# Token-major projections: the eight decode rows in float32 on four column groups of the matrix engine, and the semaphores cleared as one range

## What is computed

```
mod = silu(c) @ w_ada + b_ada                  # one row for the prompt, eight for the decode tokens
h   = rms_norm(x) * (1 + scale) + shift        # 520 x 1024
z   = h @ w_in                                 # 520 x (2048 retention + 1536 attention + 1824 RWKV + 3072 gates)
...                                            # three token mixers, gates, merge, squared-ReLU MLP
```

## Time and profile before

| what | value |
|---|---|
| time, median of 3 runs | 3102.15 us (3101.63 to 3105.66) |
| span of the profiled execution, first to last instruction | 3092.7 us |
| median run less the span | 9.45 us |
| PE busy | 2704.7 us, 87% of the span |
| DVE busy | 1464.7 us, 47% |
| ACT busy | 820.6 us, 27% |
| POOL busy | 162.0 us, 5% |

### The profile page before, as it was taken

The page is one execution under the profiler, slowest core; times in us unless marked ns, Lnnn a source line. Parts: engine busy times, 40 slices in busy tenths (PEclk is TensorE's granted clock), DMA queues, the critical chain, the costliest instruction groups (busy, mean ns, idle before and its releaser), DMA issues. The chain is left out here.

```text
span 3092.7 us, 53427 instructions
## 1 busy us (share of the span) xinstructions
PE 2704.7 (87%) x22862; PEld 2389.3 (77%) x22862; DVE 1464.7 (47%) x2073; ACT 820.6 (27%) x1218; POOL 162.0 (5%) x102
## 2 busy tenths in 40 slices
PE   5988888997698898999969879888967979799997
PEld 3777775886588698999958768567946859799997
DVE  3344346434655665334351541744366566633443
ACT  1221214223311323333222111332241114333331
POOL 0011110300000000000000210112000000000000
PEclk9997999996599799999979879999956989899999
DMA  6222345721000341222341330656010015322232
GB/s 257 98 59 58 113 134 185 228 72 52 14 3 3 126 177 66 98 82 83 137 148 35 86 120 23 219 183 200 16 52 15 3 44 178 110 83 82 83 110 109
DMA packets 216310, 305.16 MB, mean 99 GB/s; under 512 B 28021, under 2 KB 97191, under 8 KB 214786
## 3 DMA queue, kind: packets, MB, share of 16 engines
q1 hardware_dynamic: 216066, 301.67, 29.0%
HBM read 266.49 MB, written 35.14 MB: 98 GB/s over the span
## 5 line engine op out<-in xcount | busy, mean ns | idle before, releaser
L379 PE MATMUL pb<-h_high,f_high 128*128 128x260 f32 x1984 | 401.5, 284 | 4.9 <-DVEq L2619 4.9
L379 PE MATMUL pb<-h_low,f_high 128*128 128x260 f32 x1984 | 398.6, 282 | 0.0
L379 PE MATMUL pb<-h_high,f_low 128*128 128x260 f32 x1920 | 387.7, 283 | 0.0
L554 DVE TENSOR_TENSOR w_low<-ring,w_high 128x2048 fp32r<-128x2048 f32 x66 | 151.3, 2293 | 405.7 <-ACT w_high L546 404.3
L379 PEld LDWEIGHTS pb<-h_high,f_high 128*128 128x128 f32 x1984 | 306.5, 188 | 5.3 <-issue 5.3
L379 PEld LDWEIGHTS pb<-h_low,f_high 128*128 128x128 f32 x1984 | 307.6, 189 | 0.0
L554 DVE TENSOR_TENSOR f_low<-ring,f_high 128x2048 fp32r<-128x2048 f32 x60 | 137.6, 2293 | 339.1 <-ACT h_high L548 214.2
L379 PEld LDWEIGHTS pb<-h_high,f_low 128*128 128x128 f32 x1920 | 294.5, 188 | 0.0
L757 POOL TENSOR_TENSOR g_low<-yT,g_high 128x512 fp32r<-128x512 f32 x96 | 159.9, 1670 | 1978.0 <-ACT g_high L753 1978.0
L379 PE MATMUL pb<-w_high,h_high 128*128 128x512 f32 x560 | 224.9, 402 | 20.9 <-DVEq L558 11.7
L379 PE MATMUL pb<-w_low,h_high 128*128 128x512 f32 x560 | 224.2, 400 | 0.0
(11 more groups left out here) (362 smaller groups left out, 4620.2 us busy)
## 6 DMA issues: line engine op xcount, KB each, us to landing
ring<-in_w_ff_dram SPq DMA_DIRECT2D x32, 2048.0 KB, 7.8
ring<-in_w_in_dram SPq DMA_DIRECT2D x20, 2048.0 KB, 9.1
ring<-in_w_ada_dram SPq DMA_DIRECT2D x18, 2048.0 KB, 8.1
yT<-in_w_in_dram SPq DMA_DIRECT2D x96, 256.0 KB, 3.6
arena<-in_w_ada_dram SPq DMA_DIRECT2D x9, 2048.0 KB
gate_spill_dram<-yT SPq DMA_DIRECT2D x48, 260.0 KB, 4.0
arena<-gate_spill_dram SPq DMA_DIRECT2D x12, 1040.0 KB, 5.4
arena<-in_cache_k_diff_dram SPq DMA_DIRECT2D x32, 256.0 KB, 3.1
```

What stands on the lines that cost most here:

```text
L379: return PE.matmul(out, lhsT, rhs, start=start, stop=stop, skip_group_check=True)
L554: t = V.tensor_tensor(ws[n % 2][1], ring[slot][:, u * 2048:(u + 1) * 2048], ws[n % 2][0].bitcast(F32), sub)
```

## The change

The decode rows leave the five-tile loop. At the layer's start DVE puts the 8 decode columns of `h` in float32 into `h_dec`, padded to 32 columns with zeros. After the first half of each block PE makes eight float32 products of `h_dec` with the unsplit weights in the ring slot, on four column groups, into bank 4 (`dec_parts`). ACT copies bank 4 to `dec_stage`; after the second half PE sums the four groups by one float32 product with `fold` into bank 5, and ACT copies that out in place of tile 4. Since PE now reads the ring slot, DVE frees it only after `dec_parts`. The second part: `clear()` becomes one instruction over a range of 119 semaphores (two are new).

```diff
...
+        sem_numbers = sorted(s.num for s in sems.values())
+        assert sem_numbers == list(range(sem_numbers[0], sem_numbers[0] + len(sems)))
...
-                    for s in sems.values():
-                        g.sem_clear(s)
+                    g.sem_clear(range(sem_numbers[0], sem_numbers[-1] + 1))
...
+            h_dec = at(rstd, 0, KD, 32)
+            dec_count = {"made": Count(dec_made), "staged": Count(dec_staged), "read": Count(dec_made)}
...
                 dv(V.tensor_tensor(ht[:, :, SEQ:T], ht[:, :, SEQ:T], modT[:, 0:8, 1:9], add))
+                V.memset(h_dec[:, :, DEC:32], 0.0)
+                dv(V.tensor_copy(h_dec[:, :, 0:DEC], ht[:, :, SEQ:T]))
                 v.wait_ge(act_for_dve, c["dve_from_act"].next())
...
+                        def dec_parts(b):
+
+                            w = wslot(b % 2)
+                            for k in range(KD):
+                                g = slice(k % 4 * 32, k % 4 * 32 + 32)
+                                t = mm(pb[4][g, :], h_dec[:, k, :], w[:, k, :], start=(k < 4), stop=(k >= 4))
+                            t.then_inc(dec_made, 1)
+
...
-                                pe.wait_ge(act_for_pe, c["pe_from_act"].next(5))
-                                for k in range(5):
+                                pe.wait_ge(act_for_pe, c["pe_from_act"].next(4))
+                                for k in range(4):
                                     pe.wait_ge(h_ready, k + 1)
-                                    for m in range(4 if k < 4 else 0):
-                                        product(0, m, k)
-                                    if k:
-                                        t = product(0, 4, k - 1)
-                            for m in (() if before and n == 0 else range(5)):
+                                    for m in range(4):
+                                        t = product(0, m, k)
+                            for m in (() if before and n == 0 else range(4)):
...
                             if u == 0:
                                 t.then_inc(split_free, 1)
+                                dec_parts(n // 2)
+                            else:
+                                pe.wait_ge(dec_staged, dec_count["staged"].next())
+                                pe.wait_ge(act_for_pe, c["pe_from_act"].next())
+                                mm(pb[5][0:DEC, :], fold[:, 0:DEC], dec_stage).then_inc(pe_for_act, 1)
...
                                 split_hi(s, w_split, 2 * b + 2, (b + 1) % 2, 0)
+                            s.wait_ge(dec_made, dec_count["made"].next())
+                            S.activation(dec_stage, pb[4], ACT.Copy).then_inc(dec_staged, 1)
                             for m in range(5):
...
-                                                      pb[m][0:r, :], ACT.Copy))
+                                                      pb[m if m < MT else 5][0:r, :], ACT.Copy))
...
-                            split_lo(v, w_split, n, n // 2 % 2, n % 2, last=(n % 2 == 1))
+                            split_lo(v, w_split, n, n // 2 % 2, n % 2, last=False)
+                            if n % 2:
+                                v.wait_ge(dec_made, dec_count["read"].next())
+                                V.sem_inc(slot_free[n // 2 % 2], 1)
...
```

More of the change, by code:

```diff
@@ L311, in build @@
             "x_copied", "ba_made", "ba_masked", "br_made", "br_masked", "ka_made", "ka_masked", "kr_made", "kr_masked",
-            "x_made", "w_made", "w_masked", "x_added", "y_made", "y_added", "rhs_made", "rhs_copied", "u_made", "u_copied", "update_made", "state_read",
+            "dec_made", "dec_staged", "x_made", "w_made", "w_masked", "x_added", "y_made", "y_added", "rhs_made", "rhs_copied", "u_made", "u_copied", "update_made", "state_read",
             "state_done", "out_made", "out_copied")}
+        sem_numbers = sorted(s.num for s in sems.values())
+        assert sem_numbers == list(range(sem_numbers[0], sem_numbers[0] + len(sems)))
         chunk_scores, chunk_weighted, decode_added = sems["chunk_scores"], sems["chunk_weighted"], sems["decode_added"]
@@ L320, in build @@
         out_copied = sems["out_copied"]
+        dec_made, dec_staged = sems["dec_made"], sems["dec_staged"]
         pe_for_dve, dve_for_pe = sems["pe_for_dve"], sems["dve_for_pe"]
@@ L801, in build, with token_major @@
             upper = ((4, 5), (6, 7))
-            def token_major(col0, n_blocks, n_split, gates=False, before=None):
+            def token_major(col0, n_blocks, n_split, dec_stage, gates=False, before=None):
                 with nc.Block() as block:
@@ L918, in heads_to_columns @@
                 return pe_part, dve_part
-            token_major(RET0, 4, 1, gates=True, before=(start_sp, start_pe, start_s, start_v))
+            token_major(RET0, 4, 1, y_raw[:, 0:512], gates=True, before=(start_sp, start_pe, start_s, start_v))
             Z = lambda b: at(arena, b * 2560, 5, 512)
@@ L1125, in _ @@
                     pe_part(pe)
-            token_major(DIFF0, 3, 0)
+            token_major(DIFF0, 3, 0, x_raw[:, 0:512])
             w_ada_rest = L("w_ada")[:, 4 * 512:12 * 512]
```

## The result

Beside runs of the kernel before on the same chip, the changed kernel takes 3055.98 us (median of 4 runs, 3050.3 to 3057.57) against 3103.9 us (4 runs): ratio 0.9863, interval 0.9844 to 0.9883. It is faster, by 48 us. The forecast was 62.4 us less; the ratio laid on the 3102.15 us that the forecast started from gives 3059.6, outside 3029 to 3056. The ratios are given as recorded, and they are not the quotients of the medians: here that would be 0.9846, by which the time is 3054.3, just inside the range. In the other comparisons the two are up to 4 us apart. So the time missed narrowly, and a difference of under some 5 us can't be read from one comparison.

The account below looks back on a forecast made before the run. PE, busy for 87% of a 3092.7 us span, was taken as the bound, plus clears with nothing beside them. Terms -25.2 - 78.1 + 25.9 + 14.0 + 1.0 = -62.4 us took 3102.15 to 3040 us; range 3029 to 3056.

Parts of the forecast that it names:

- The clears: Three places of semaphore clears: one range clear each at 0.1 us instead of 8.6, 8.5 and 8.3; 25.2 us less.
- The tile removed: Decode tile in `token_major`: 24 products gone in each of 14 blocks, 5.58 us a block, 78.1 us less.
- `dec_parts`: Eight float32 products on column groups after each first half: 1.85 us x 14, 25.9 us more.
- that rival: Column groups don't overlap in `dec_parts`: 7.4 us each, +78 us over 14 blocks, 3118 and slower; 3%.
- The sum of the groups: One float32 product after each block's second half: 1.0 us x 14, 14.0 us more (12.9 to 15.7).
- Switching between the two forms: PE's changes around `dec_parts` and sum: taken as nothing, at most 4.8 us; by the skill's rule nearer 3044 than 3040.
- DVE at a layer's start: One more memset and copy before `h` is finished: 0.5 us x 2, 1.0 us more, at most 0.6 a layer.
- Costed at nothing: In `token_major`, ACT's 0.60 us staged copy, DVE's and PE's new waits and the later-freed ring slot: no time added.
- The base: Whole kernel: median run 9.45 us above the span, untouched by edits, so 3102.15 us is the starting time.
- Nothing later gives it back: Stages after the edited ones: each starts at a barrier with transfers issued behind it, so the gain of 62.4 us stays.
- up to 6 us either way: PE's clock after pauses some 8 us shorter, at two layer starts and the last block; within the 80% forecast.
- its last sentence: Signs of being wrong: block over 26 us, clears' gap staying, or untouched stages moving over a few us through PE's clock.

Follow-up runs that it names:

- dec_first_split_sum: dec_first with the sum of the four groups made as two split products instead of one float32 product; 0.9784 and again 0.9781 of the kernel before.
- dec_first: The changed kernel with `dec_parts` moved ahead of each block's first half; 3030.28 us against 3096.16 for the kernel before, ratio 0.9775.

## Why the prediction missed

Point by point, by its own steps:

- *The clears*: 25.2 us forecast, 23.4 measured. "I take 0.1 us" for one range clear was the step; it is 0.68. The price that the Trainium skill's "Runtime: NRT & Kernel Launch" gives in its section on the preamble, about 1.2 us for zeroing the user semaphores, was about as far above it as mine was below; how many semaphores that price is for, no run here shows.
- *The tile removed*: right. Tiles 2.79 us apart, 1344 products.
- *`dec_parts`*: right, 1.86 us at a granted clock of 1.00; the columns overlap behind split products, and that rival falls.
- *The sum of the groups*: right within its bounds, 0.96 us against 1.0.
- *Switching between the two forms*: "I take nothing" was wrong. Four steps make 0.41 us a block, 5.7 us over 14; the bound of 4.8 was near. The Trainium skill's rule in "TensorEngine Tiling (Array Packing)", key properties, that a change of tiling mode drains the engine, spoke for the dearer sum, and the steps around `dec_parts` are what it would give. But the trace doesn't single out the tiling: the float32 sum, 8 columns and no groups, has the same steps, the same 8 columns as split products have none ahead of them (dec_first_split_sum, 101.19 to 101.43), and float32 column groups start 0.01 us behind the float32 sum (dec_first, 101.51 and 101.52). All rows fit a cost of changing between split and float32 products; which of the two makes it was not tested by itself.
- *DVE at a layer's start*: 0.63 us where it was 0.26, 0.37 a layer against 0.5. The timeline of DVE after, with the two new instructions in the middle:

```profile
74.34 0.22 DVE L729 TENSOR_TENSOR yT<-yT,modT 128x64 f32<-128x64 f32 x1
74.67 0.22 DVE L730 MEMSET rstd<- 128x192 f32 x1
74.81 0.13 DVE L731 COPY rstd<-yT 128x64 f32<-128x64 f32 x1
74.97 1.00 DVE L736 TENSOR_SCALAR yT<-yT,coef,modT 128x512 f32<-128x512 f32 x2
```

- *Costed at nothing*: right for ACT's staged copy, the waits and the ring slot. No load is late in `token_major`.
- *The base*: "the median run stands 9.45 us above the span, and no edit touches what lies around it". Only 1.8 us lie around it, in every run. The other 7.6 us are an execution shorter than the median run, no constant to be added. By itself this shifts no difference, but it hid how far the untouched stages move.
- *"Nothing later gives it back"*: this is the step that failed by most. The decode part gives back 8.3 us on the mean in stages that it doesn't touch. 4.7 of it lie in the two norm stages: fewer PE instructions move PE's fetches, one falls among full loads, the loads come late, and PE's last products there run at the lower clock. Moving the fetch moved these stages; the rest stays open. The step reasoned from the barriers and the transfers that the program issues, and left out what is fetched across them. The forecast allowed "up to 6 us either way", in other places and for another reason, and no rival said it, though its last sentence named untouched stages that move "through PE's clock" as a sign of being wrong.

In sum: -62.4 forecast; -57.1 in the edited stages, of the difference 5.7 in the switches and 1.8 in the clears, less 2.2 us in terms that came out smaller (0.6 of it the sum of groups, 0.3 DVE; the rest I did not trace); and 9.2 us given back in the comparison with the result, which leaves 48. Without what was given back the time would have been 3045 (3102.15 less 57.1), inside the range.

## What to carry to other kernels

Sum the direct terms by the stages that they stand in, and set the sum against the median run, not against one profile; then look at the stages that no edit touches, over several profiles, before calling a difference there chance. Price each step of PE between split and float32 products at some 0.1 us, and put float32 work on column groups where PE waits anyway: that was worth more here than the sum of groups. Where a kernel loses or gains PE instructions inside a loop, look where the instruction fetches now fall among its full transfers; here that was worth some 2 us in one stage of each layer, and the whole time did not show it.

## What the hardware showed that was not expected

- A range clear costs some 5.4 ns a semaphore over about 40 ns: 0.677 us for 119, 0.044 for one; single clears start 73 ns apart.
- Float32 column-group products into one bank start beside a float32 product of another form (101.51 and 101.52) and share 2.67 us with it, less than the 2.82 of both apart.
- Where a fetch of 16 KB of PE's instructions falls is worth some 2.4 us on the mean in a stage that the change doesn't touch (28.7 us over ten stages, 31.1 over 22), about half of it the later weights and the rest the granted clock of its last products: 0.93 or 0.83 over the stage in layer 0 of the changed kernel.
- 199 semaphore increments on PE held up its first product by 17.0 us (14.32 to 31.35), beyond the wait that was there: they start some 0.15 us apart, though each is listed with 51 ns.
